# One more pass of an expert loop gets its row numbers from TensorE, and its gather is issued earlier

## The reference, cut to what matters

```
g_sel = argmax(x @ w_gr + b_gr)                      # one of 4 groups of 4 experts
top_p, top_i = top_k(softmax(e_logits[g_sel]), 2)    # two experts in that group
y = sum over the two of gate * (silu(x @ w_gate[e]) * (x @ w_up[e])) @ w_down[e]
out = layer_norm(ALPHA * x + y)
```

## Time and profile before

| | |
|---|---|
| median of three runs | 646.45 us |
| profiled execution, its own time | 650.46 us |
| its span, first to last instruction | 648.6 us |
| PE busy | 615.8 us, 95% of the span |
| DVE, POOL, ACT busy | 366.7, 204.6, 164.4 us |
| mean granted clock of TensorE | 0.988 |

### The profile page before, as it was taken

One profiled execution on the slowest core, in us unless ns is written; L12 is line 12 of the kernel. 1 busy time (PEld: TensorE's weight loads), 2 busy tenths in 40 slices (PEclk: granted clock), 3 DMA queues, 4 the chain that ended last, 5 costly groups with the idle time before them and its releaser, 6 DMA issues.

```text
span 648.6 us, 8964 instructions
## 1 busy us (share of the span) xinstructions
PE 615.8 (95%) x3319; PEld 394.6 (61%) x3319; DVE 366.7 (57%) x845; ACT 164.4 (25%) x367; POOL 204.6 (32%) x248
## 2 busy tenths in 40 slices
PE   6899999999999979999999999999999999999992
PEld 3588788887888854446888784454574443333230
DVE  1485898326556863557653874257885342443465
ACT  1175211002544120002001740221433111212144
POOL 7050010100677735312000986011324731110221
PEclk9999999999999989999999999999999999999997
DMA  8995678616335354003904985354998999999898
GB/s 278 364 312 171 235 169 229 240 51 211 118 94 214 130 195 148 16 0 107 348 1 128 340 310 200 134 225 161 369 415 326 406 411 366 334 411 418 323 185 162
DMA packets 49175, 150.08 MB, mean 231 GB/s; under 512 B 5498, under 2 KB 8250, under 8 KB 44897
## 3 DMA queue, kind: packets, MB, share of 16 engines
q1 hardware_dynamic: 35159, 112.48, 46.6%
q0 software_dynamic: 11232, 31.76, 17.4%
q10 hardware_dynamic: 2738, 5.23, 2.1%
HBM read 131.83 MB, written 21.90 MB: 237 GB/s over the span
## 4 chain that ended last, share of the span: by engine, by line
PE 74%; DMA 12%; DVE 7%; POOL 2%; issue 2%; SPq 2%; ACT 1%; DVEq 0%; POOLq 0%; ACTq 0%
PE ps L611 14%; PE ps L788 14%; PE ps L609 9%; PE ps L1148 7%; PE ps L517 5%; PE ps L1168 4%; DMA xn<-in_x_sample 2%; PE ps L807 2%; PE ps L890 2%; PE ps L584 2%; PE ps L874 2%; DMA xn<-y_d 1%; DMA P<-x_d,smp 1%; SPq L1273 1%; DMA wring<-in_ca_wq 1%
## 5 line engine op out<-in xcount | busy, mean ns | idle before, releaser
L788 PE MATMUL ps<-wring,P 128*128 128x512 f32 x224 | 99.2, 596 | 0.0
L788 PEld LDWEIGHTS ps<-wring,P 128*128 128x128 f32 x224 | 41.6, 190 | 49.1 <-issue 49.0
L1926 DVE SCALAR_TENSOR_TENSOR P<-ps,P 128x256 f32<-128x256 f32 (+1 forms) x83 | 33.8, 424 | 57.2 <-PE ps L611 36.6
L1148 PE MATMUL ps<-wring,P 128*32 128x512 f32 (+1 forms) x320 | 63.6, 593 | 0.9 <-DVE P L2600 0.9
L517 PE MATMUL ps<-xT,wring 128*128 128x312 f32 (+1 forms) x256 | 57.4, 383 | 0.0
L517 PEld LDWEIGHTS ps<-xT,wring 128*128 128x128 f32 x256 | 46.4, 190 | 9.3
L2600 DVE COPY P<-ps 128x512 f32<-128x512 f32 x10 | 6.9, 692 | 63.5 <-PE ps L1129 63.5
L1148 PEld LDWEIGHTS ps<-wring,P 128*32 128x32 f32 (+1 forms) x320 | 20.4, 122 | 31.0 <-issue 30.9
L2922 POOL TENSOR_TENSOR P<-P,xT 128x2048 f32<-128x2048 f32 x8 | 36.0, 4521 | 9.2 <-DMA xT<-sq_d 5.4
L2774 POOL TENSOR_SCALAR rstd<-agg 128x1 f32<-128x1 f32 (+1 forms) x10 | 12.0, 1195 | 85.3 <-DVE agg L1856 85.3
L2234 DVE SCALAR_TENSOR_TENSOR xn<-xn,ps 128x512 f32<-128x512 f32 x16 | 11.0, 684 | 42.1 <-PE ps L788 31.1
(11 more groups left out here) (480 smaller groups left out, 1157.1 us busy)
## 6 DMA issues: line engine op xcount, KB each, us to landing
wring<-in_w_in SPq DMA_DIRECT2D x5, 2048.0 KB, 9.7
wring<-in_w_gate SPq DMA_DIRECT2D x10, 1024.0 KB, 8.3
wring<-in_w_up SPq DMA_DIRECT2D x10, 1024.0 KB, 11.2
P<-in_w_down SPq DMA_DIRECT2D x10, 1024.0 KB, 11.6
P<-in_cache_mem_k SPq DMA_DIRECT2D x8, 1024.0 KB, 7.0
P<-in_cache_mem_v SPq DMA_DIRECT2D x8, 1024.0 KB, 4.9
y_d<-P POOLq DMA_DIRECT2D x1, 4160.0 KB, 32.1
wring<-in_ca_wv SPq DMA_DIRECT2D x2, 2048.0 KB, 20.0
```

The lines of the kernel that those rows point to most:

```text
L788: last = mm(bk[:, :], src[:, k, START[t]:START[t] + TR], w[:, k, :], start=(k == 0), stop=(k == KC - 1))
L1148: last = mm(GU[p % 2][lo:lo + m, :].rearrange("p (g f) -> p g f", g=2), xgT[:, p % 3, k, lo:lo + m], gu[s][:, :, k, :], start=(k == 0), st ...
L1926: V.scalar_tensor_tensor(dst, src, scale, part, ALU.mult, ALU.add).then_inc(part_added, 1)
```

## The change

NPICK becomes 4, so `picks_later` holds a third set of 0/1 matrices (for pass 3), `pick_tokens` makes 15 matmuls where it made 10, `early_rows` has three columns, and the small products that find the first experts' columns are 64 wide where they were 48 (128 where they were 96, for the last two tiles together). gather(3) is issued on POOL behind the list scatters and ahead of the wait for them; it still waits for `xgT_full` of pass 0, but no longer for a list. The list loads go in the order 4, 0, 1, 2, 3, 5, and the shared count of `idx_in` is 64 in place of 48, so that the result of each of the passes 0 to 3 waits for four lists.

```
-NPICK = 3
+NPICK = 4
...
-            return (idx_in, 16 * NPICK) if p < NPICK else (lists_in[p % 3], 16 * (p // 3))
+            return (idx_in, 16 * NPICK) if p < NPICK else (lists_in[p % 3], 16 * len(range(NPICK + (p - NPICK) % 3, p + 1, 3)))
...
                 if p >= 3:
                     pool.wait_ge(xgT_full, 2 * (p - 2))
+                if p >= NPICK:
                     pool.wait_ge(*entry_landed(p))
...
-            for p in range(1, NPICK):
-                gather(p)
+            gather(1)
+            gather(2)
             for n in range(SAMPLES, NT):
                 scatter_lists(n)
+            gather(3)
             pool.wait_ge(lst_out, 16 * 2 * NT)
...
             pool.wait_ge(sorted_ready, INDEXED)
-            list_load(3)
-            for p in (0, 1, 2, 4, 5):
+            for p in (4, 0, 1, 2, 3, 5):
                 list_load(p)
-            gather(3)
             norm_vectors("ln3_g", "ln3_b")
```

## The result

| | before | after |
|---|---|---|
| median, all runs of this comparison | 648.81 us (22 runs, 645.25 to 655.04) | 651.42 us (22 runs, 648.93 to 654.13) |
| ratio | | 1.0042, 95% interval 1.0026 to 1.0058 |
| profiled execution: span | 648.6 us | 649.4 us |
| mean granted clock, profiled execution | 0.988 | 0.985 |

The change made the kernel slower, by 0.42% (2.7 us), where 0.45 us less was forecast. The 22 runs put the kernel before at 648.81 us, so the three runs behind the forecast's base of 646.45 were low ones; carried to that base by the ratio, the outcome is 646.45 * 1.0042 = 649.2 us.

The account below looks back on a forecast made before the run. The prediction took TensorE, with PE busy for 95% of the span, as the bound. Its terms, -1.53 + 0.79 + 0.29 = -0.45 us, took the median of 646.45 to 646.0 us, range 645.2 to 647.5.

Parts of the forecast that it names:

- The stall at turn_rows(3): TensorE's idle wait for gather(3)'s data at turn_rows(3) would go whole with the gather issued earlier: -1.53 us.
- Picks on DVE: Four more picks and wider operations on DVE would make TensorE start pick_tokens later: +0.79 us, between 0.7 and 1.4.
- products, +0.29: Five more matmuls in pick_tokens on TensorE, at most 0.059 us each, would delay pass 0 by 0.29 us.
- covers for the earlier tiles: Added DVE work for tiles 0 to 2 would be hidden by idle times of 0.67 and 0.57 us: nothing.
- The handover of 0.06 us: From the end of the last pick on DVE to TensorE's start of pick_tokens: some 0.06 us, at most 0.37.
- What TensorE does after an idle spell is not a term: Matmuls after idle time would take their usual time, as down's eight did at 3.60 us behind 1.53 us idle: nothing.
- The new wait for four lists: Results of passes 0 to 3 waiting for four lists would cost nothing, with 1.2 us to spare on ACT.
- the 512.8 to 514.6 that I gave: Sign of a right forecast: ACT's first scaled result would come between 512.8 and 514.6.
- the rival of the late list: Pass 3's list lands late, queued behind gather(3), and down(1) starts late: +4.05 us, 650.5 us; chance 0.09.
- The two readings of the queue's order: Small list loads either queue behind gather(3), the first list landing no sooner than it, or pass it with no delay.
- 647.5: Range's upper end, from a rival where turn_rows(3) still waits and only costs remain, up to +1.08 us; chance 0.05.

Follow-up runs that it names:

- e2: Changed kernel with pick_tokens swapped behind the second pick_rows and the wait for the early rows moved ahead of pass 1; ratio 0.9959 to before.
- e8: The e2 kernel with the list loads in the old order 3, 0, 1, 2, 4, 5; ratio 1.0022 to before.
- e10: The e2 kernel measured once more, on another chip; ratio 1.0002 to before.
- e11: The e2 kernel with pick_tokens between the two parts of the second pick_rows; ratio 0.9971 to before.
- e6: Changed kernel with gather(3) back behind the list loads; ratio 1.0067 to before.
- e9: The changed kernel measured once more, on another chip; ratio 1.0071 to before.
- e4: Kernel before with fifteen products in pick_tokens in place of ten, nothing else changed; ratio 1.0000 to before.
- e5: Kernel before with only pick_tokens put behind the second pick_rows and the wait for the early rows ahead of pass 1; ratio 1.0047 to before.
- e7: The e2 kernel with gather(3) back behind the list loads; ratio 1.0050 to before.
- e3: Kernel before with four more unread pick-like operations on DVE ahead of the last pick, so TensorE gets the picks late; ratio 1.0036 to before.

## Why the prediction was wrong

- **The stall at turn_rows(3), -1.53 us.** Right: gone in the changed kernel, e2, e8, e10 and e11. By starts of rows it was worth 1.69. gather(3) went at 495.01 and landed 9.1 us later. But e6 shows that in the changed kernel the stall would have gone without the move of the gather.
- **Picks on DVE, +0.79, and products, +0.29.** Right to a few hundredths: pick_tokens starts 0.78 us later against `late_normaliser`, and the second pick_rows follows 0.88 us behind it where it was 0.59. Four more picks at 0.257 us, and covers for the earlier tiles, as the rows of before gave them. The handover of 0.06 us, for which no row stood, came out: the last pick ends at 484.18 + 0.33 = 484.51, and TensorE starts at 484.57. One reading was wrong and cost nothing: in before pick_tokens starts 2.7 us ahead of the first gate_up (485.28 against 488.0), not half a microsecond; that is its distance to the second pick_rows.
- **"What TensorE does after an idle spell is not a term: behind the 1.53 us of idle the eight matmuls of down took their usual 3.60 us."** This is the step that failed. The term is +3.26 us. I took one idle spell as a sample of all. The one ahead of turn_rows(3) has full float32 matmuls on both sides; the new one has fifteen products of two columns behind it. Both of my additions, the wait and the products, went to the same quiet place, and I priced each as time alone. (Two one-column groups of `late_normaliser` and the small counts stand ahead of it as well; whether they count was not tested.) The clock column of the windows over this place in the trace of before reads 1.00 and gives no warning; that the wait and the products would lie in one piece was to be seen.
- **The new wait for four lists.** Right: nothing. In the changed kernel ACT never waited for a list: its first scaled result, at 511.42, waited for TensorE's late down(0). That this is 512.9 on before's clock of events, inside the 512.8 to 514.6 that I gave, is luck. The test is e11, where the passes are on time. ACT got the lists at 512.55, with the next exp at 514.79:

```profile
512.55 0.69 ACT L1760 ACTIVATE P<-ps,smp 128x512 f32<-128x512 f32 x1 [7.91 <-DMA smp<-lst_d,smp]
514.79 0.39 ACT L1747 ACTIVATE P<-ps 128x256 f32<-128x256 f32 x1 [1.55 <-PE ps L1147]
```

  On before's clock of events that is 513.5, inside the range. The six list loads behind gather(3), issued from 500.8 on, landed after 4.4 to 5.8 us in the changed kernel: the rival of the late list didn't come. The two readings of the queue's order aren't told apart by it: gather(3) had landed by 495.01 + 9.1 = 504.1, before the first list could, at 500.85 + 4.4.
- **The range.** 647.5 was the end at which the change earns nothing and costs all its terms. The outcome, 649.2 on that base, lies above it, because a term of 3.3 us was missing, not because one was mis-sized. The rival that was missing is "the clock falls": a wait and small products in one place, with 2.2 + 7.1 us of full matmuls behind it that would run at half speed for as long as the fall lasts.
- The sum without that term is confirmed as nearly as the runs allow: e2, e8 and e10, with the change's picks, products, gathers and no fall of the clock in their profiles, have stretches 1.28 to 1.44 us under before's (-1.24 expected for the swap).

## What to carry to other kernels

Before adding a wait or tiny matmuls to TensorE, see whether the two, old and new, end up side by side, and price the full matmuls behind that place at half speed as a rival. Let full matmuls cover a late operand, so that the wait is gone when the tiny ones come. Here that took moving one call and one wait, and on the chip where both were measured it turned 0.7% lost (e9) into 0.3% gained (e11, measured once). Busy time hides the clock, so compare a group's duration with its twins, and read the granted clock by stretch.

## What the runs showed of the hardware

- TensorE dropped to its lower level though the trace shows it 100% busy ahead of the fall (e4: fifteen products of 2 columns, 0.06 us each, then full matmuls, and the fall about 1 us later). It stayed low, with TensorE busy, for 3 us (e5, e7), 7 us (the changed kernel, e4) or 10 us (e3, from 485.5 to past 495.5).
- A stall that grows can cost more than itself: 1.53 us of idle ahead of turn_rows(3) left the clock at 1.00 in the kernel before, 3.74 us in e5 cost another 1.7 us in down(1).
- The same instructions meet a fall in some executions and not in others, and not by the length of the idle time alone. Near 31 us, in a part that no variant touches, the profile of before has 2.18 us of idle time and then eight matmuls at the lower level; after and e2 run the same eight at the higher one, e2 behind 2.40 us:

```profile
31.97 3.58 PE L609 MATMUL ps<-wring,P 128*128 128x256 f32 x8 [2.18 <-DVE wring L1901]
```

```profile
31.30 1.99 PE L609 MATMUL ps<-wring,P 128*128 128x256 f32 x8 [1.42 <-DVE wring L1901]
```

```profile
31.41 1.99 PE L609 MATMUL ps<-wring,P 128*128 128x256 f32 x8 [2.40 <-DVE wring L1902]
```

  Before's profile lost 1.6 us there, about the head start that the profile after has at 477; that the one comes of the other isn't shown. This place falls in 3 of the 14 profiles (before, e8, e10). Another, behind some 3 us of idle time near 232 us, falls in 12 of 14 (not in e2 and e5). So the mean clock of one run doesn't say at which place it was lost.
- Clocks of the kernel before reach from 0.982 to 0.995 over 95 runs, its times from 646.1 to 653.9 us. The Trainium skill, "TensorE: Matmul & The Clock Gate", Part 1 on the clock gate, says that the gate's setting follows how busy the engine has been recently. It also says that the number of slow matmuls at the start of one and the same kernel differs from run to run. On the first, e4 adds that the busy time of the profile doesn't show what brings a fall; the second holds here in the middle of a kernel too, as at 31 us.
- Open: what exactly the small products and the idle time each add to a fall; only one execution of each kernel has a trace by stretch.
